# Three chunks abreast in a recurrent scan: a new order of steps, some products of the next chunk on GpSimd, part of the residual kept in DRAM meanwhile

## The reference, cut to what matters

```python
def _rwkv7_scan(S0, r, w, k, v, kk, a):
    def step(S, inp):
        r_t, w_t, k_t, v_t, kk_t, a_t = inp
        sa = jnp.einsum('bhvk,bhk->bhv', S, kk_t)
        S = (S * w_t[:, :, None, :] - sa[..., None] * (kk_t * a_t)[:, :, None, :]
             + v_t[..., None] * k_t[:, :, None, :])
        return S, jnp.einsum('bhvk,bhk->bhv', S, r_t)
...
    yf_c, Sf_c = _rwkv7_scan(S0, r_c, wf_c, k_c, v_c, kk_c, a_c)
    yb_c, Sb_c = _rwkv7_scan(S0, *_flip_seq(r_c, wb_c, k_c, v_c, kk_c, a_c))
    yf_l, _ = _rwkv7_scan(Sf_c, r_l, wf_l, k_l, v_l, kk_l, a_l)
    yb_l, _ = _rwkv7_scan(Sb_c, *_flip_seq(r_l, wb_l, k_l, v_l, kk_l, a_l))
```

## Time and profile before

| | us |
|---|---|
| median of 3 runs | 4312.69 (4312.33 to 4316.23) |
| the profiled execution | 4314.55 (span 4312.8) |
| TensorE busy | 3819.4 (89%) |
| VectorE busy | 2118.5 (49%) |
| ScalarE busy | 1416.6 (33%) |
| GpSimd busy | 32.1 (1%) |
| the scan, 2409 to 2741 us | 332 (8% of the span) |

### The profile page before, as it was taken

How to read it: one execution, slowest core, us unless ns; L and a number is a source line. 1 busy time by engine, 2 the same in 40 slices (tenths; PEclk the granted TensorE clock), 3 DMA queues, 4 the chain that set the end, 5 groups by cost and what they waited for, 6 DMA issues and landing times. The chain is left out here.

```text
span 4312.8 us, 67312 instructions
## 1 busy us (share of the span) xinstructions
PE 3819.4 (89%) x27854; PEld 3112.8 (72%) x27854; DVE 2118.5 (49%) x3453; ACT 1416.6 (33%) x2565; POOL 32.1 (1%) x52
## 2 busy tenths in 40 slices
PE   7989999998889999969888588789999899668998
PEld 5767777767767777758666477678888788567887
DVE  5575644434765644441554655543332426574334
ACT  3333532223334422231443233332222223363222
POOL 0000000000000000000000000000000000000000
PEclk8999999999999999979999799999999999789999
DMA  5341444433333444411011000111221120002332
GB/s 156 88 103 52 152 143 147 166 106 99 97 79 94 143 149 163 160 45 45 1 49 39 3 4 4 48 49 59 64 64 58 49 79 30 1 20 79 97 97 78
DMA packets 312373, 340.85 MB, mean 79 GB/s; under 512 B 23680, under 2 KB 289696, under 8 KB 305568
## 3 DMA queue, kind: packets, MB, share of 16 engines
q1 hardware_dynamic: 311424, 332.59, 24.1%
q10 hardware_dynamic: 672, 4.36, 0.4%
HBM read 316.48 MB, written 20.45 MB: 78 GB/s over the span
## 5 line engine op out<-in xcount | busy, mean ns | idle before, releaser
L274 DVE TENSOR_TENSOR weights_lo<-weight_ring,weights_hi 128x1024 fp32r<-128x1024 f32 x371 | 454.4, 1225 | 1375.1 <-ACT weights_hi L270 1375.1
L270 ACT ACTIVATE weights_hi<-weight_ring 128x1024 fp32r<-128x1024 f32 x371 | 392.8, 1059 | 1605.1 <-PE banks L321 1533.9
L321 PE MATMUL banks<-mlp_x_lo,weights_hi 128*128 128x512 f32 (+1 forms) x1280 | 479.8, 375 | 0.0
L321 PE MATMUL banks<-mlp_hidden_hi,weights_hi 128*128 128x512 f32 (+1 forms) x1280 | 476.9, 373 | 0.0
L321 PE MATMUL banks<-mlp_hidden_lo,weights_hi 128*128 128x512 f32 (+1 forms) x1280 | 476.3, 372 | 0.0
L321 PE MATMUL banks<-mlp_hidden_hi,weights_lo 128*128 128x512 f32 (+1 forms) x1280 | 475.7, 372 | 0.0
L321 PE MATMUL banks<-normed_hi,weights_hi 128*128 128x512 f32 (+1 forms) x1040 | 360.8, 347 | 21.8 <-ACT normed_hi L288 19.7
L321 PE MATMUL banks<-mlp_x_hi,weights_hi 128*128 128x512 f32 x768 | 307.4, 400 | 20.9 <-DVE mlp_x_lo L305 9.5
L321 PE MATMUL banks<-mlp_x_hi,weights_lo 128*128 128x512 f32 x768 | 304.9, 397 | 0.0
L321 PEld LDWEIGHTS banks<-mlp_hidden_hi,weights_hi 128*128 128x128 f32 x1280 | 241.1, 188 | 51.6 <-issue 6.7
L321 PEld LDWEIGHTS banks<-mlp_x_lo,weights_hi 128*128 128x128 f32 x1280 | 242.8, 190 | 44.7
(11 more groups left out here) (552 smaller groups left out, 6994.9 us busy)
## 6 DMA issues: line engine op xcount, KB each, us to landing
weight_ring<-in_w SPq DMA_DIRECT2D x64, 1024.0 KB, 5.3
mod_chunks<-in_mod_w SPq DMA_DIRECT2D x24, 2048.0 KB, 9.8
weight_ring<-in_w_in SPq DMA_DIRECT2D x42, 1024.0 KB, 5.4
weight_ring<-in_w_up SPq DMA_DIRECT2D x32, 1024.0 KB, 5.6
weight_ring<-in_w_down SPq DMA_DIRECT2D x32, 1024.0 KB, 5.1
weight_ring<-in_w_in SPq DMA_DIRECT2D x52, 512.0 KB, 4.3
weight_ring<-in_w_out SPq DMA_DIRECT2D x16, 1024.0 KB, 5.2
gate_logits_dram<-gates_staged SPq DMA_DIRECT2D x48, 256.0 KB, 4.5
```

Source lines behind the costliest of these rows:

```text
L270: act.activation(self.w_hi[:, t % 2], self._raw(t), ACT.Copy).then_inc(self.w_rounded, 1)
L274: dve.tensor_tensor(self.w_lo[:, t % 2], self._raw(t), self.w_hi[:, t % 2].bitcast(F32), ALU.subtract)\
L321: mm = pe.matmul(bank, a[:, k, :], b[:, k, t0:t0 + w], start=(k == 0 and n == 0), stop=(k == KD - 1 and n == 2))
```

## The change

The list `order` is rewritten. It describes a period in which three chunks of a direction are at work: the levels of chunk i, the preparation of chunk i + 1 (`grow`, `bend`, `cross`, `start`, `join`, `mask`, and now also `turn`, `token_major` and a separate copy `v`), and the finish of chunk i - 1 (`g`, `solve` and the output and state products, `u`, `push`, `state`, `y`). Products of the finish and of the preparation are put into free quarters of apply 1 to 3; the old steps `solve`, `state`, `out` are no entries of the list any more, and `push` is a new one. There are 14 periods for each direction, -1 to 12, where there were 13. `kr`, `scored`, `kb_tok` and `v_tok` exist twice, the chunk's last decays three times, `grow` and the solution have tiles of their own. `bend` and `bend_rest` are GpSimd's, `g` is ScalarE's. `cross` and `start` use banks a and b in place of c and d. For the added tiles six rows of the residual `x2` are given up during the scan as well: ten rows go to DRAM and come back, the last six of them after the weight fetch, and a tile `rw_extra` of 1024 floats is added.

The diff, cut to its core (of changed functions only the new form stands where it is long):

```diff
-            for c in range(4):
-                sp.dma_start(kept[c], aside[:, c, :]).then_inc(set_aside, 16)
+            for place, row in zip(kept, aside):
+                sp.dma_start(place, row).then_inc(set_aside, 16)
             sp.wait_ge(loaded, 64)
-            sp.wait_ge(set_aside, 64)
+            sp.wait_ge(set_aside, 16 * len(aside))
...
+    dirs = [Dir(), Dir()]
+    for t in dirs:
+        t.scored = [take(2, 8).rearrange("p h (q m) n -> p h q (m n)", m=2) for _ in range(2)]
+    for t in dirs:
+        t.kb = take(12).rearrange("p (q m) n -> p q (m n)", m=3)
+    for t in dirs:
+        t.kr = [take(8).rearrange("p (q m) n -> p q (m n)", m=2) for _ in range(2)]
+        t.first, t.zx = take(2, 4), take(2, 4)
+        t.kb_tok = [take(2, 4) for _ in range(2)]
+    for d, t in enumerate(dirs):
+        t.v_tok = [take(4) for _ in range(2)]
+        t.yl = [None] + [take(4) for _ in range(5)]
+        t.solution, t.grow, t.state, t.g0, t.u = (take(4) for _ in range(5))
...
+        t.bearer, t.first_bearer = small[:, d:d + 1], small[:, 2 + d:3 + d]
+        t.ends = [small[:, 4 + 12 * d + 4 * e:8 + 12 * d + 4 * e] for e in range(3)]
...
-    order = [("pe", "apply", 1, 0), ("dve", "keep", 1, 0), ("pe", "turn", 0, 0), ("pe", "grow_by", 1, 0),
-             ("act", "token_major", 0, 0), ("act", "merge", 1, 0)]
-    for l in range(2, 5):
-        order += [("pe", "apply", l, 0), ("dve", "keep", l, 0), ("pe", "grow_by", l, 0), ("act", "merge", l, 0)]
-    order += [("pe", "apply", 5, 0), ("act", "grow", 0, 1), ("dve", "keep", 5, 0), ("pe", "grow_by", 5, 0),
-              ("dve", "g", 0, 0), ("act", "merge", 5, 0), ("dve", "bend", 0, 1), ("pe", "solve", 0, 0),
-              ("act", "u", 0, 0), ("dve", "bend_rest", 0, 1), ("pe", "state", 0, 0), ("pe", "out", 0, 0),
-              ("dve", "state", 0, 0), ("pe", "cross", 0, 1), ("act", "y", 0, 0), ("dve", "start", 0, 1),
-              ("pe", "join", 0, 1), ("dve", "mask", 0, 1)]
+
+    order = [("pe", "apply", 1), ("dve", "keep", 1), ("act", "g", 0), ("pe", "grow_by", 1), ("act", "merge", 1),
+             ("pe", "apply", 2), ("dve", "keep", 2), ("act", "u", 0), ("act", "grow", 0), ("pool", "bend", 0),
+             ("pe", "grow_by", 2), ("act", "merge", 2), ("pe", "push", 0), ("dve", "state", 0), ("pool", "bend_rest", 0),
+             ("pe", "apply", 3), ("dve", "keep", 3), ("act", "v", 0), ("act", "y", 0),
+             ("pe", "grow_by", 3), ("act", "merge", 3), ("pe", "cross", 0), ("dve", "start", 0),
+             ("pe", "apply", 4), ("dve", "keep", 4), ("pe", "grow_by", 4), ("act", "merge", 4),
+             ("pe", "join", 0), ("dve", "mask", 0),
+             ("pe", "apply", 5), ("dve", "keep", 5), ("pe", "grow_by", 5), ("act", "merge", 5),
+             ("pe", "turn", 0), ("act", "token_major", 0)]
     lag = len(order) // 2
...
+        own = [(on, name, l, period) for period in range(-1, turns + 1) for on, name, l in order]
...
+            def apply(t, l, i):
+                level, tail, front = there(i), there(i - 1), there(i + 1)
                 x = t.first[:, 1] if l == 1 else t.zx[:, 1]
+                scored = t.scored[i % 2]
+                old, new = (i - 1) % 2, (i + 1) % 2
+                old_scored = t.scored[old]
+                if level and l == 1:
+                    pe.wait_ge(t.started, i + 1)
+                    pe.wait_ge(t.masked, i + 1)
+                if level and l > 1:
+                    pe.wait_ge(t.merged[l - 1], i + 1)
+                if tail and l == 1:
+                    pe.wait_ge(t.token_major, i)
+                    pe.wait_ge(t.v_copied, i)
+                    pe.wait_ge(t.merged[5], i)
+                if tail and l == 2:
+                    pe.wait_ge(t.g_copied, i)
+                    done(i, t.token_major)
+                    if not level:
+                        done(i - 2, t.added)
+                        done(i - 2, t.y_copied)
+                for q, h, half, other in heads():
+                    if level:
+                        mm = one(t.d[half, 1, q, :], scored[other, h, q, 0:64], x[other, q, :])
+                        if (q, h) == (3, 1):
+                            mm.then_inc(t.applied[l], 1)
+                    if tail and l == 1:
+                        one(t.c[half, 1, q, :], old_scored[half, h, q, 0:64], t.v_tok[old][half, q, :], start=q == 0)
+                    if tail and l == 2:
+                        one(t.a[half, 0, q, :], t.kb_tok[old][half, h, q, :], t.v_tok[old][half, q, :], start=q == 0)
+                    if front and l == 3:
+                        at = offset(t, i + 1) + 1
+                        mm = one(t.c[half, 1, q, :], f[half, RW_V + q, at:at + 64], same[half, :])
+                        if (q, h) == (3, 1):
+                            mm.then_inc(t.v_turned, 1)
+                if tail and l == 1:
+                    done(i - 2, t.decayed)
+                    if i == 1:
+                        pe.wait_ge(t.emptied, 1)
+                    for q, h, half, _ in heads():
+                        mm = one(t.c[half, 1, q, :], t.kr[old][half, q, 0:64], t.state[half, q, :], start=False)
+                    mm.then_inc(t.gathered, 1)
+                if tail and l == 2:
+                    for q, h, half, other in heads():
+                        mm = one(t.c[other, 1, q, :], t.solution[half, q, :], t.g0[half, q, :])
+                        if (q, h) == (3, 1):
+                            mm.then_inc(t.solved, 1)
+                        one(t.b[half, 0, q, :], t.v_tok[old][half, q, :], old_scored[half, h, q, 64:P], start=q == 0)
+                if tail and l == 3:
+                    pe.wait_ge(t.state_made, i)
+                    for q, h, half, other in heads():
+                        mm = one(t.b[half, 0, q, :], t.u[other, q, :], old_scored[other, h, q, 64:P], start=False)
+                    mm.then_inc(t.out_made, 1)
+
+            def grow_by(t, l, i):
                 if l == 1:
+                    done(i - 1, t.g_copied)
                 if l == 2:
+                    done(i - 1, t.u_copied)
+                if l == 3:
+                    done(i + 1, t.v_copied)
+                if there(i):
+                    z = t.first[:, 0] if l == 1 else t.zx[:, 0]
+                    pe.wait_ge(t.kept[l], i + 1)
                     for q, h, half, other in heads():
+                        mm = one(t.c[half, 0, q, :], t.yl[l][half, q, :], z[half, q, :])
+                        if l < 5:
+                            mm = one(t.d[other, 0, q, :], z[half, q, :], t.yl[l][half, q, :])
+                    mm.then_inc(t.grown_by[l], 1)
+
+            def step(t, name, l, i):
+                if name == "apply":
+                    apply(t, l, i)
+                elif name == "grow_by":
+                    grow_by(t, l, i)
+                elif name == "push" and there(i - 1):
+                    old = (i - 1) % 2
+                    pe.wait_ge(t.u_copied, i)
                     for q, h, half, other in heads():
+                        one(t.b[half, 0, q, :], t.state[half, q, :], t.kr[old][half, q, 64:P], start=False)
+                        mm = one(t.a[half, 0, q, :], t.kb_tok[old][other, h, q, :], t.u[other, q, :], start=False)
+                    mm.then_inc(t.state_made, 1)
+                elif name == "cross" and there(i + 1):
+                    kr = t.kr[(i + 1) % 2]
+                    pe.wait_ge(t.bent, i + 2)
+                    done(i - 1, t.added)
+                    done(i - 1, t.y_copied)
+                    for q, h, half, other in heads():
+                        one(t.a[half, 0, q, :], t.kb[half, q, 64:P], kr[half, q, 0:64])
+                        mm = one(t.b[other, 0, q, :], kr[half, q, 0:64], t.kb[half, q, 64:P])
                     mm.then_inc(t.crossed, 1)
+                elif name == "join" and there(i + 1):
+                    kr = t.kr[(i + 1) % 2]
+                    pe.wait_ge(t.rest_bent, i + 2)
+                    pe.wait_ge(t.started, i + 2)
                     for q, h, half, _ in heads():
+                        mm = one(t.ab[:, h, q * P:(q + 1) * P], t.kb[half, q, 64 * h:64 * h + P], kr[half, q, :])
                     mm.then_inc(t.joined, 1)
+                elif name == "turn" and there(i + 1):
+                    pe.wait_ge(t.masked, i + 2)
                     for q, h, half, _ in heads():
+                        mm = pe.transpose(t.ab[:, h, q * 64:(q + 1) * 64], t.kb[half, q, 64 * h:64 * h + P], same[half, :])
                     mm.then_inc(t.turned, 1)
 
...
+                elif name == "v" and there(i + 1):
+                    act.wait_ge(t.v_turned, i + 2)
+                    act.activation(t.v_tok[(i + 1) % 2], t.c[:, 1], ACT.Copy).then_inc(t.v_copied, 1)
+                elif name == "token_major" and there(i + 1):
+                    act.wait_ge(t.turned, i + 2)
```

(54 more changed lines are left out.)

189 lines of the change are left out of this document (37 added, 152 removed).

## The result

| kernel | median us (lowest to highest) | profiled execution, us | span, us |
|---|---|---|---|
| before, timed beside it | 4316.23 (4312.33 to 4319.43) | | |
| after | 4288.25 (4280.5 to 4297.59) | 4288.21 | 4286.4 |

The ratio is 0.9938 with an interval of 0.9927 to 0.995: faster by some 27 us. I had forecast 57 to 60 us, 4255.5, with its own range up to 4274. The direction holds, and less than half of the gain came.

A forecast was written before the change was run, and what follows sets the result against it. Scan bound by TensorE waiting for VectorE and ScalarE copies; halves of 10.75 us, edges included and DRAM at 0, take 57 to 58 us off 4314.55: about 4257, median 4255.5. Own range 4241 to 4274; with rivals 4233 to 4288.

The forecast's parts named there:

- the walk: Scan half-period reckoned step by step, products in free quarters costing nothing: 11.02 us new, 13.61 old against 13.32 measured.
- The correction: Scan half-period: 2 to 3% taken off the reckoned 11.02 us, giving 10.75, because the old order reckoned 2% long.
- the 9.0 us of the old order: Scan: TensorE cost of the 16 steps of one chunk and direction, leaving 4.3 us of each half as waiting.
- The waits: Scan: the gain must come from TensorE's waits; idle gaps of 0.6 to 0.8 us remain before grow 4 and 5.
- ScalarE's g and v copies: Scan: ScalarE's queue makes grow 3 and grow 1 wait 0.27 and 0.28 us for these copies.
- Bends: Scan, on GpSimd: 0.71 us each (0.42 to 1.7), ending before cross and join, so the move costs nothing.
- Edges: Scan's start and end: first apply 1 at 2415.0, end at 2683.7, 58 us less, some 5 us of doubt.
- DRAM: Six more residual rows written during preparation and restored during the finish: cost 0, bounds 0 and 8 us.
- (a): Rival, scan: VectorE and GpSimd collide, costing 5 to 32 us, middle 15: 4271, up to 4288; chance 0.18.
- (b): Rival, scan: waits close further, a half of 9.8 us, 23 us below the forecast, 4233; chance 0.10.
- (c): Rival, scan: GpSimd's bends become the bound; at 3.2 us each 67 us above the old, 4380; chance 0.04.
- (d): Rival, scan: the three stages don't overlap, a half stays near 13.3 us, time about 4315; chance 0.04.

The follow-up runs named there:

- e1: Kernel after without three sets of eight products riding in free quarters (apply 1, apply 2, solve), 96 instructions a half: 4261.76 us, ratio to before 0.9874.
- e3: Kernel after plus 16 useless products (64 instructions) a half in free quarters of apply 4 and 5: 4315.82 us, ratio to before 1.0004.
- e8: Kernel after without three rider sets and six of every eight products that turn V, 120 instructions a half fewer: 4258.09 us, ratio to before 0.9865.
- e4: Kernel after with the five bends back on VectorE at the same places of the list: 4296.83 us, ratio to before 0.9957.
- e6: Kernel after with v and u stacked, one 128-row product replacing two over 64 rows, 64 instructions a half fewer: 4357.05 us, ratio to before 1.01.

## Why the prediction was half right

- **The step that failed is the TensorE term of the walk.** It priced every step by its products in the array, 0.46 to 0.50 us whether two or four quarters work, and so riders at nothing; "TensorE issue unchanged at 8.6 us a half" was the line in the prediction. The half came out at 12.39 us where the walk had 11.02 and the forecast 10.75. What the runs showed in its place: breaks of 1.54 us a half, each of which ends a steady time after an instruction packet, 46 ns for each rider by e1 and, with 64 more instructions a half, 27.6 us by e3. Without the breaks the half of after is 10.85 us. It was to be asked of the trace of before: 56 packets in the same window, none closer than 3.27 us, 1.7 us of issue stalls. I had counted the 8.6 us as a lower bound without asking for a second one. A half of 848 instructions is 3.3 packets, at the least interval of 3.3 us 10.9 us. That alone would not have given the result, since it lies under the walk's 11.02; it says only that an order of 10.75 us a half asks for packets as fast as they were ever seen to come.
- **The correction** of 2.5% that I took off the walk, because the old order came out 2% shorter than it, is neither borne out nor refuted: 10.85 lies between 10.75 and 11.02. Without it the sum would have been 24.5 x 0.27, some 7 us higher: 4262. That e8 has 11.09 us is no confirmation of 11.02, since 0.63 of it are breaks.
- **A slip in a sum**: the 9.0 us of the old order count five steps on two quarters, where its list has four (apply 1, solve, state, out). It is 8.6, the same as the new order's, so 4.7 us of the old half were waits and not 4.3. The forecast doesn't use it.
- **The waits** closed nearly as the walk says: mask out of the list, merge at 3.6 us instead of 17.3, keep 35 times in the window. Keep's waits have two sizes. 18 are of 0.6 us, before grow 4; with the 0.2 us from the last issue to the last result, which the walk counts in, they are its 0.8. The other 17, before grow 5, are of 0.18, and so 0.4 where the walk had 0.6. ScalarE's g and v copies, which I expected as releasers of grow 1 and grow 3, don't appear in the window: TensorE comes later than they do.
- **Bends**: 0.69 to 0.73 us against 0.71. Off the path, as said. Moving them is worth some 9 us by the medians of e4, not clear of its interval, which the forecast didn't price by itself.
- **Edges**: the first apply 1 is at 2414.00 instead of 2415.0; the end of the scan is 2716.0, against 2683.7 forecast. With the measured half, the sum of the prediction would give 2415.0 + 25 x 12.39 - 0.1 = 2724.7, so the edges came out 9 us better than reckoned, where I had put some 5 us of doubt. The masks say where: the first four are at 2412.10, 2420.98, 2429.92 and 2440.38 us and the fifth at 2452.81, so the first three halves take 8.9, 8.9 and 10.5 us. In the first two no direction has an older chunk to finish, in the third one has, and the sum, made from full halves, hardly allowed for that. So 25 halves that are 1.64 us longer than forecast, 41 us, less these 9 are the 32 us by which the scan ends later than forecast.
- **DRAM**: nothing seen, as said. In ScalarE's timeline of after the split of the output product's input starts 26.5 us earlier than in the earlier trace rows, as much as the scan's end moved, 25.6, and a little more:

```profile
2758.02 4.50 ACT L280 ACTIVATE out_x_hi<-mixed 128x768 fp32r<-128x768 f32 x6
```

- **Rivals**: (a) is refuted by the keep rows and by e4; its upper number for the total, 4288, came near by accident. (b), (c) and (d) didn't happen: the overlap works, and five bends, 3.5 us, are far from filling GpSimd's half of 12.39.

What stays open: why the packets come 3.7 us apart on average and not at the 3.3 of the closest pair, in stretches where TensorE is starved. No run separates the fetch's own latency from a fetch that was asked for late. Nor is it known why e8 still has breaks with 120 instructions a half fewer.

## What to carry to other kernels

When TensorE runs many small products, count instructions as well as array time, four to an f32 product of 64x64, and multiply the packets they fill by the closest spacing that the trace shows between instruction packets. That is a floor, and stalls begin above it: here the floor was 10.9 us, and a half that would have been 10.85 took 12.39. "Issue" stalls in the middle of a step that end 2.2 to 2.9 us after such a packet are the sign. A free quarter of the array doesn't make a rider free, and a reckoning tested on an order full of waits says nothing of a cost that those waits hide. One product over 128 rows in place of two over 64 saves instructions, if products of one kind are kept together.

## What the hardware showed that I had not expected

- Instruction packets of 16,384 bytes never start closer than 3.3 us in the scan, 13 ns an instruction, while a step issues at 7 ns. All 29 issue stalls of the window end 2.20 to 2.76 us after one.
- Changing between products over 64 and over 128 rows costs some 0.23 us each time: 4.1 us for a push of 32 records that alternates. In e6, where every push does so, the granted clock also fell to its lower level for 3.4 us six times in 223 us.
- Semaphore waits on TensorE that are already met follow each other every 106 ns (each record is 51 ns long): 1.7 us for 16, eight times an instruction's share of the feed.
